# Three gate units inside the last retention chunk, row sums of the down weights on VectorE, and the tail's diagonals earlier

## The reference

```
h = x + W_out( sig(g_A) * Ret(RMSNorm(x)) + sig(g_B) * MLA(RMSNorm(x)) )
h = h + (silu(g) * u) @ w_down,  g, u = split(RMSNorm(h) @ w_gate_up)      # D_FF = 2816
y = RMSNorm(h) * norm_final_w
```

## Time and profile before

| | |
|---|---|
| median of 3 runs | 2051.46 us (2051.01 to 2053.17) |
| the profiled execution | 2048.32 us, its span 2046.5 us |
| TensorE (PE) busy | 1968.6 us, 96% |
| VectorE (DVE) / ScalarE (ACT) / GpSimd (POOL) busy | 1367.6 / 831.7 / 621.8 us |
| mean granted TensorE clock | 0.985 of full |
| chain that ended last | PE 81%, DVE 12%, issue 3%, ACT 2% |
| DMA | 276.29 MB, 135 GB/s mean |

### The profile page before, as it was taken

The page is one execution under the profiler, slowest core; times in us unless marked ns, Lnnn a source line. Parts: engine busy times, 40 slices in busy tenths (PEclk is TensorE's granted clock), DMA queues, the critical chain, the costliest instruction groups (busy, mean ns, idle before and its releaser), DMA issues.

```text
span 2046.5 us, 35899 instructions
## 1 busy us (share of the span) xinstructions
PE 1968.6 (96%) x14476; PEld 1900.1 (93%) x14476; DVE 1367.6 (67%) x2020; ACT 831.7 (41%) x1426; POOL 621.8 (30%) x470
## 2 busy tenths in 40 slices
PE   8999999999999989899999979999999999999997
PEld 8978888889989989899999979999999999999997
DVE  6567776765666556866668896756556565686775
ACT  6334445442222235455554425633333333333342
POOL 0110000001345442225133232144444444370342
PEclk9999999999999989999999989999999999999998
DMA  8301010152354565854755543222323222564322
GB/s 315 113 25 33 25 33 25 32 207 64 122 175 158 170 242 190 297 187 159 243 205 209 182 136 131 78 77 91 107 80 112 91 97 100 198 243 170 109 83 88
DMA packets 112724, 276.29 MB, mean 135 GB/s; under 512 B 13232, under 2 KB 29552, under 8 KB 106032
## 3 DMA queue, kind: packets, MB, share of 16 engines
q1 hardware_dynamic: 112560, 273.99, 38.2%
HBM read 188.79 MB, written 85.16 MB: 134 GB/s over the span
## 4 chain that ended last, share of the span: by engine, by line
PE 81%; DVE 12%; issue 3%; ACT 2%; DMA 1%; POOL 1%; SPq 0%; DVEq 0%; ACTq 0%; POOLq 0%
PE ps L1209 24%; PE ps L1210 24%; PE ps L1211 24%; PE ps L1304 1%; PE ps L1402 1%; DVE tmp L2297 1%; DVE negmax L2519 1%; DVE t_lo L2290 1%; PE ps L1310 1%; PE ps L1518 1%; PE ps L1465 1%; DVE pt_lo L2290 1%; PE ps L1461 1%; PE ps L1462 1%; DVE s_lo L2290 1%
## 5 line engine op out<-in xcount | busy, mean ns | idle before, releaser
L1209 PE MATMUL ps<-s_hi,t_hi 128*128 128x272 f32 x1344 | 393.1, 292 | 20.4 <-DVE s_lo L2290 19.4
L1210 PE MATMUL ps<-s_hi,t_lo 128*128 128x272 f32 x1344 | 391.2, 291 | 0.0
L1211 PE MATMUL ps<-s_lo,t_hi 128*128 128x272 f32 x1344 | 389.9, 290 | 0.0
L1209 PE MATMUL ps<-sx_hi,t_hi 128*128 128x272 f32 x1232 | 357.3, 290 | 3.0 <-ACT p L2106 2.5
L1210 PE MATMUL ps<-sx_hi,t_lo 128*128 128x272 f32 x1232 | 357.2, 290 | 0.0
L1209 PEld LDWEIGHTS ps<-s_hi,t_hi 128*128 128x128 f32 x1344 | 256.9, 191 | 23.0 <-DVE s_lo L2290 13.4
L1210 PEld LDWEIGHTS ps<-s_hi,t_lo 128*128 128x128 f32 x1344 | 256.7, 191 | 0.0
L1211 PEld LDWEIGHTS ps<-s_lo,t_hi 128*128 128x128 f32 x1344 | 256.7, 191 | 0.0
L1211 PE MATMUL ps<-sx_lo,t_hi 128*128 128x272 f32 x880 | 255.5, 290 | 0.0
L1209 PEld LDWEIGHTS ps<-sx_hi,t_hi 128*128 128x128 f32 x1232 | 234.9, 191 | 3.4 <-issue 3.3
L1210 PEld LDWEIGHTS ps<-sx_hi,t_lo 128*128 128x128 f32 x1232 | 234.5, 190 | 0.0
(11 more groups left out here) (281 smaller groups left out, 4883.4 us busy)
## 6 DMA issues: line engine op xcount, KB each, us to landing
t_row<-in_weights SPq DMA_DIRECT2D x48, 512.0 KB, 5.9
s_raw<-s_x SPq DMA_DIRECT2D x21, 1088.0 KB, 5.7
w_stage<-in_weights SPq DMA_DIRECT2D x35, 512.0 KB, 3.9
s_y<-hg SPq DMA_DIRECT2D x44, 272.0 KB, 2.1
d_raw<-s_y SPq DMA_DIRECT2D x7, 1632.0 KB, 8.9
raw<-in_weights SPq DMA_DIRECT2D x22, 512.0 KB, 4.4
hg<-in_weights SPq DMA_DIRECT2D x22, 512.0 KB, 4.6
d_raw<-s_y SPq DMA_DIRECT2D x7, 1360.0 KB, 6.0
```

Source lines behind the costliest of these rows:

```text
L1209: nc.tensor.matmul(out, wh, xh, start=start, stop=False, skip_group_check=onto)
L1210: nc.tensor.matmul(out, wl, xh, start=False, stop=False, skip_group_check=onto)
L1211: return nc.tensor.matmul(out, wh, xl, start=False, stop=stop, skip_group_check=onto)
```

## The change

Four edits in one.

1. `retention_steps` puts three gate units U of octet 0 into the last head: U0 after Z(6), U1 and U2 after Z(7), ahead of Z(8). In the first two octets the units use other bank pairs (`octet_banks`: 3, 0, 2, 1 for p = 0 to 3). The roundings of their weights and operand are spread over chunks 4 to 8 on ScalarE and VectorE, the first operand is loaded one chunk earlier, the weight rows 3 and 1 are loaded half by half, and the last state is stored before the last transposed tile.
2. In the last gate-up pair ScalarE rounds the first down operand after p5's copy instead of before it, and SyncE issues that operand's load before the pair's stores and the residual's load after the second operand's.
3. The down weights' sums T3, T2, T4, T1 go from GpSimd to VectorE, inside its loop; the operand of step 1 is split before the loop.
4. In the tail VectorE makes the diagonals before accumulations that stood ahead of them, and the scalings are spread between the accumulations.

```diff
@@ retention_steps
         if c:
             steps.append(("Z", c - 1))
+        if head + 1 == RH and c == 7:
+            steps.append(("U", 0))
     steps += [("F", *unit) for unit in fill]
+    if head + 1 == RH:
+        steps += [("U", 1), ("U", 2)]
     return steps + [("Z", 8)]
...
+        def octet_banks(o, p):
+            b = 2 * ((3, 0, 2, 1)[p] if o in (GATE_RET, GATE_A) else p)
+            return ps[:, b:b + 2, 0:QUARTER]
@@ first_loads, SyncE
-                elif c == 6:
+                elif c == 5:
...
-                    for r in (3, 1):
-                        for half in range(2):
+                    for half in range(2):
+                        for r in (3, 1):
                             row_load(0, r, half)
@@ SyncE, last head
+                        if s[1] == 8:
+                            sp.wait_ge(state_f, 9 * h + 9)
+                            sp.dma_start(o["state_s"][:, h, :], s_sample[h % 2][:, :]).then_inc(state_out[h % 2], 16)
                         sp.wait_ge(zt_copy, n + 1)
...
@@ SyncE, after the pairs
+                    sp.wait_ge(q_done, last + 1)
+                    down_operand_load(0)
                 gated_store(pair)
...
             down_operand_load(1)
+            for p in range(4):
+                sp.wait_ge(h_out[p], H_OUT + 64)
+            residual_load(C11)
@@ octet_unit, TensorE: banks of units 0 to 3 of octet 0 are free when
                 elif s == 0:
                     if p == 0:
+                        pe.wait_ge(p_free, own[-1])
+                    elif p == 1:
                         pe.wait_ge(sc_mid, 9 * RH)
                         pe.wait_ge(z_copy, 9 * RH)
-                    elif p == 1:
-                        pe.wait_ge(zt_copy, 9 * RH)
-                        pe.wait_ge(kd_copy, 9 * RH)
                     elif p == 2:
                         pe.wait_ge(state_f, 9 * RH)
                     else:
-                        pe.wait_ge(p_free, own[-1])
+                        pe.wait_ge(zt_copy, 9 * RH)
+                        pe.wait_ge(kd_copy, 9 * RH)
@@ ScalarE: weights of units 0, 1 after B(4), B(5), of 2, 3 after B(8); operand parts after A(7) and Z(5)
+                if n >= 9 * RH - 5 and n != 9 * RH - 3 and n != 9 * RH - 2:
+                    weights_octet({9 * RH - 5: 0, 9 * RH - 4: 1, 9 * RH - 1: 2}[n])
                 if n == 9 * RH - 1:
+                    weights_octet(3)
@@ VectorE: low halves after B(5), B(6), B(8), N(8); the operand's after N(6)
+                        if n in (9 * RH - 4, 9 * RH - 3, 9 * RH - 1):
+                            weights_octet_low({9 * RH - 4: 0, 9 * RH - 3: 1, 9 * RH - 1: 2}[n])
@@ ScalarE, last pair
                 part(p5, pair, "Z")
...
+                elif not more:
+                    for part_of in range(2):
+                        down_operand_high(0, part_of)
@@ VectorE, down
+            for part_of in range(3):
+                down_operand_low(1, part_of)
             for u in range(LAST_STEP):
+                g, n = divmod(u, UNITS)
+                if n < 4:
+                    down_sums(g, "T3", n)
+                    down_sums(g, "T2", n)
+                if 8 <= n < 12:
+                    down_sums(g, "T4", n - 8)
+                if 13 <= n < 17:
+                    down_sums(g, "T1", n - 13)
@@ VectorE, tail (the new order)
+            accumulate_part(0, 1)
             final_diagonal(0)
+            accumulate_part(0, 2)
+            final_scale(0, 0)
             accumulate_part(0, 3)
...
+            accumulate_part(1, 1)
+            final_scale(0, 5)
+            final_diagonal(1)
+            final_scale(0, 6)
+            accumulate_part(1, 2)
...
+            accumulate_part(1, 3)
+            for t in range(2, 5):
                 final_scale(1, t)
+            final_diagonal(2)
```

More of the change, by code:

```diff
@@ L1146, in gated_store @@
                         operand_store(6, e, y_s4)
+            last = 7 * (UP_PAIRS - 1)
             for pair in range(UP_PAIRS - 1):
@@ L1424, in _, with octet_unit @@
                         last.then_inc(p_done, 1)
+            def octet_unit(o, s, p):
+                n, j = UNITS * o + 4 * s + p, STEPS * o + s
+                opens = s in OPENING_STEPS
+                pe.wait_ge(ot_low, n + 1)
+                if s == 0 and o:
+                    pe.wait_ge(o_read, reads_until(o - 1, 4 * C12 + ((1, 3, 2, 0)[p] if o == GATE_B else p)))
+                elif s == 0:
+                    if p == 0:
+                        pe.wait_ge(p_free, own[-1])
+                    elif p == 1:
+                        pe.wait_ge(sc_mid, 9 * RH)
+                        pe.wait_ge(z_copy, 9 * RH)
+                    elif p == 2:
+                        pe.wait_ge(state_f, 9 * RH)
+                    else:
+                        pe.wait_ge(zt_copy, 9 * RH)
+                        pe.wait_ge(kd_copy, 9 * RH)
+                elif s < 4:
+                    pe.wait_ge(o_copy, 12 * o + 4 * (s - 1) + p + 1)
+                elif s == 4 and o in GATES:
+                    pe.wait_ge(c_act, 16 * o + p + 1)
+                else:
+                    pe.wait_ge(o_read, reads_until(o, 4 * (s - 4) + p))
+                th, tl = t_hi[n % 4], t_lo[n % 4]
+                for half in range(2):
+                    cols = slice(QUARTER * half, QUARTER * (half + 1))
+                    for k in range(4):
+                        if p == 0 and half == 0 and k % 2 == 0:
+                            pe.wait_ge(so_low, 2 * j + k // 2 + 1)
+                        last = product(octet_banks(o, p)[:, half, :], th[:, k, :], tl[:, k, :],
+                                       s_hi[j % 3][:, k, cols], s_lo[j % 3][:, k, cols], k == 0 and opens, k == 3, not opens)
+                last.then_inc(oct_done, 1)
             for h in range(RH):
@@ L1474, in _ @@
                         last.then_inc(zt_done, 1)
[L1478 to L1488, removed]
-                    elif p == 1:
-                        pe.wait_ge(zt_copy, 9 * RH)
-                        pe.wait_ge(kd_copy, 9 * RH)
-                    elif p == 2:
-                        pe.wait_ge(state_f, 9 * RH)
-                    else:
-                        pe.wait_ge(p_free, own[-1])
[L1496 to L1507, removed]
-                        last = product(ps[:, 2 * p + half, 0:QUARTER], th[:, k, :], tl[:, k, :],
-                                       s_hi[j % 3][:, k, cols], s_lo[j % 3][:, k, cols], k == 0 and opens, k == 3, not opens)
-                last.then_inc(oct_done, 1)
             def square_sums(i):
@@ L2195, in _ @@
                     weights_high(n, "B")
-                else:
-                    for part_of in range(2):
-                        down_operand_high(0, part_of)
                 act.wait_ge(q_done, 7 * pair + 4)
@@ L2605, in _ @@
                                                 rstd[0:L, n % 2, :], ALU.subtract, ALU.mult).then_inc(z_norm, 1)
-            for part_of in range(2):
-                operand_octet_low(0, part_of)
+                        if n == 9 * RH - 1:
+                            weights_octet_low(3)
+                        if n == 9 * RH - 3:
+                            for part_of in range(2):
+                                operand_octet_low(0, part_of)
             def weights_low(pair, step):
@@ L2831, in down_weights_low, with down_sums @@
                     d_weights(dw_hi, u).rearrange("p k c -> p (k c)")).then_inc(dw_low, 1)
+            def down_sums(g, name, p):
+                b11, b12, b21, b22 = [d_rows[r][p // 2][:, p % 2, 0:DOWN_GROUPS[g] * P] for r in range(4)]
+                if name == "T3":
+                    for r in (1, 3):
+                        dve.wait_ge(row_in[r][p // 2], 16 * (OCTETS + g + 1))
+                    nc.vector.tensor_tensor(b12, b22, b12, ALU.subtract).then_inc(dw_sum, 1)
+                elif name == "T2":
+                    dve.wait_ge(dw_low, UNITS * g + p + 1)
+                    dve.wait_ge(dw_sum, dw_sum_at(g, "T3", p))
+                    nc.vector.tensor_tensor(b11, b12, b11, ALU.add).then_inc(dw_sum, 1)
+                elif name == "T4":
+                    dve.wait_ge(row_in[2][p // 2], 16 * (OCTETS + g + 1))
+                    dve.wait_ge(dw_low, UNITS * g + 8 + p + 1)
+                    dve.wait_ge(dw_sum, dw_sum_at(g, "T2", p))
+                    nc.vector.tensor_tensor(b12, b21, b11, ALU.subtract).then_inc(dw_sum, 1)
+                else:
+                    dve.wait_ge(dw_low, UNITS * g + 4 + p + 1)
+                    dve.wait_ge(dw_sum, dw_sum_at(g, "T4", p))
+                    nc.vector.tensor_tensor(b11, b22, b11, ALU.subtract).then_inc(dw_sum, 1)
             def down_operand_low(j, part_of):
@@ L2968, in final_scale @@
                                                    ps[:, 2 + 2 * i, 0:QUARTER], ALU.mult, ALU.mult).then_inc(scaled, 1)
+            for part_of in range(3):
+                down_operand_low(1, part_of)
```

(4 more changed lines are left out.)

96 lines of the change are left out of this document (32 added, 64 removed).

## The result

The changed kernel takes **2035.82 us** (median of 4 runs, 2034.43 to 2037.54), the kernel before, beside it on the same chip, 2052.32 us (4 runs, 2051.01 to 2054.84). The profiled executions stand closer: 2037.54 us (span 2035.7, clock 0.986) against 2048.32 (2046.5, 0.985), 10.8 us.

The account below looks back on a forecast made before the run. TensorE was taken to bound the kernel, leaving only its holes and half clock to win. Gains of 1.0 + 2.5 + 4.4 + 4.3 = 12.2 us from 2051.46 gave 2039.3 us, range 2034.5 to 2045.

Parts of the forecast that it names:

- signs of being wrong: Copy starting after 764, sums above 1.5 us, new TensorE wait at down units 3 to 6, over one new half-clock stretch.
- Part 1: Retention into first octet: unit 4 ends 2.1 us sooner, minus 1.1 us half clock; 1.0 us gained (1.5 lost to 4).
- What bounds, and the price of half clock: Whole kernel: TensorE busy 1968.6 of 2046.5 us; only holes and half clock winnable; 3.41 us busy half clock costs 1.55.
- rival A: Retention: its hole comes back whole before unit 4 with more half clock, worth -1.5 us, total 2041.8; chance 0.14.
- Part 2: Last gate-up pair: p5 copied once its bank is full, operand load issued earlier; 2.5 us gained (2.0 to 2.6).
- Part 3: Down stage: row sums on VectorE remove a 2.9 us wait and 1.5 us of clock; 4.4 us gained (1 to 4.5).
- B: Down stage: VectorE's sums are hindered by late rows, gain shrinks to 0 or 1 us, total 2043.3; chance 0.10.
- D: Down stage: VectorE becomes the bound; sums of 2.5 us eat all 12.2 us, at 2.9 total 2057; chance 0.03.
- Part 4: Tail: earlier diagonals save 2.25, 1.28 and 0.3 us of waits, plus 0.5 us of clock; 4.3 us gained (3 to 5).
- the base: Whole kernel before the change: median 2051.46 us, from which the forecast gain was subtracted.

Follow-up runs that it names:

- two experiments: Changed kernel with the whole retention edit taken back: 2034.74 us, ratio 0.991; kernel before with the retention edit alone: 2053.94 us, ratio 1.0004.
- the two experiments on it: Changed kernel with operand and weights rounded ahead of the quadrant copy: 2037.03 us; the same with the last store between units 1 and 2: 2034.75 us.

## Why the prediction was nearly right

The time lies in the range, but two of the prediction's own signs of being wrong came: the copy began after 764 (764.69), and there is more than one new half-clock stretch (767.43, 1276.01, 1293.08). Part 1 and the two stretches gave less than forecast and parts 2 to 4 more, and that these nearly cancel in the profiles (10.8 us against 12.2) is luck.

**What bounds, and the price of half clock.** Right. Each hole that came back in the down stage brought a stretch of 3.41 us of half clock, and cost its own length plus some 1.5 us there: 2.73 + 1.55 and 2.62 + 1.55 (positions differ by 4.4 us in both). In their profiles both cost 1.6 us more in the tail, which no term of the sum has: what is undone in one stage can move the half clock of a later one.

**Part 1, +1.0 forecast, -0.6 by the profile, nothing by two experiments.** The mechanism was right step by step. Unit 0 was forecast at 746.7 and started at 748.02, of which 1.1 us is from before the edit. From there unit 0 took 3.2 us rather than 3.0 and chunk 8 with the transposes behind it 2.1 rather than 1.5, so the last transposed block was stored at 760.27, 0.8 us late. ScalarE's rows:

```profile
759.73 0.52 ACT L1972 ACTIVATE zt<-ps,gains 128x64 f32<-128x64 f32 x2 [5.26 <-PE ps L1521]
764.69 0.62 ACT L2032 ACTIVATE hg<-ps 128x544 f32<-128x544 f32 x1 [4.44 <-DMA yr_spill<-zt]
```

The store took 3.9 us, near my 3.6. The copy was forecast at 762.0 and came at 764.69, past the bound of 764, of which again 1.1 is older. The term that was mis-sized is the clock's, "I charge 1.1 us for it (0 to 3)": it was 5.71 x 0.454 = 2.6 us. A stop that I expected at the operand's second half didn't come (0.18 us), which hid most of the late copy. That the hole has the forecast 4.8 us is luck: the copy is late, but so is unit 3, and the first low half takes 1.28 us instead of the 2.28 of before, since GpSimd's sums are over by 766.5. This is rival A in kind. I named the queue behind the copy but had its price wrong: by the two experiments on it, the store is only one of two covers, the other being VectorE's halves beside GpSimd at 2.4 us.

**Part 2, +2.5 forecast.** The wait for `p` is gone. The step's reasoning gave the gain to "p5 copied as soon as its bank is full". The runs give it to the load: with the load early the order on ScalarE is worth nothing, and without it the new order loses 3.6 us in the profile. ScalarE's last pair, the answer to the earlier trace rows:

```profile
1779.83 0.63 ACT L2124 ACTIVATE p<-ps 128x544 f32<-128x544 f32 x1 [2.37 <-PE ps L1223]
1780.35 2.10 ACT L2148 ACTIVATE d_hi<-d_raw 128x1088 fp32r<-128x1088 f32 x2
```

**Part 3, +4.4 forecast, 7.4 together with part 2 against 6.9.** Right. VectorE's rows in the down stage, where the earlier trace rows stood, and the tile of the rows:

```profile
1802.67 0.95 DVE L2861 TENSOR_TENSOR d_row<-d_row,d_row 128x768 f32<-128x768 f32 x1
1803.72 0.96 DVE L2865 TENSOR_TENSOR d_row<-d_row,d_row 128x768 f32<-128x768 f32 x1
1804.60 0.95 DVE L2310 TENSOR_TENSOR dw_lo<-d_row,dw_hi 128x768 fp32r<-128x768 f32 x1
1805.47 0.71 DVE L2973 TENSOR_TENSOR hg<-hg,ps 128x544 f32<-128x544 f32 x1
```

```profile
L2310 DVE TENSOR_TENSOR dw_lo<-d_row,dw_hi x56: 816/884/2111, 1786.3 to 2006.3; 128x768 fp32r<-128x768 f32 x28, 128x640 fp32r<-128x640 f32 x28
...
L2861 DVE TENSOR_TENSOR d_row<-d_row,d_row x8: 815/884/951, 1799.2 to 1928.3; 128x768 f32<-128x768 f32 x4, 128x640 f32<-128x640 f32 x4
```

A sum costs 0.95 us of 0.96 forecast, a unit 3.43 of 3.6. Rivals B and D needed 2.5 us or a late row; neither came. The experiment with the operand in the loop shows that the step named as an aside, the split before the loop, is needed as much as the move of the sums.

**Part 4, +4.3 forecast, 6.8 by position, 5.5 by the experiment.** The waits went as forecast, with a little more at the third diagonal:

```profile
2028.59 0.72 PE L1649 MATMUL ps<-fin_diag,ones 128*128 128x272 f32 x2 [1.23 <-DVE fin_diag L2992]
```

2.25 + 1.28 + (1.92 - 1.23) = 4.2 us against my 2.25 + 1.28 + 0.3. The clock was mis-sized: I let the drop of 2016.88 stay and gave it back 0.5 us; there was none before 2030.36, worth 4.57 x 0.454 = 2.1. In before it began ahead of the hole, which is why I kept it. That part 4 alone took it away isn't shown: with the new tail it came back in the two runs that undid half of part 3.

**The base and the sum.** From profile to profile the gain is 10.8 us, 1.4 less than forecast; from median to median it is 16.5, 4.3 more, of which 0.9 is the base (2051.46 was shown, 2052.32 measured beside the result; later comparisons gave 2052.3 to 2053.2). Undone one at a time, the parts cost 0 or less (part 1), 3.8 (part 2's load), 4.8 to 6.4 (part 3) and 5.5 us (part 4), medians against the 2036.26 of the changed kernel, each good to 1 or 2 us: 14 to 16 of some 16.5. The surplus over the forecast thus lies in parts 2 to 4, mostly, it seems, in the half clock that goes with their holes. Open: why the changed kernel has the half clock at 1276 and 1293.

## What to carry to other kernels

A hole before a unit has as many causes as there are queues that end near it: before an edit is priced, write down when each of them would be ready with the first removed. Here 2.2 us off the store bought 1.5 us at most, inside the spread, and with the operand's place in three queues it bought 5 us. Price a hole with the clock behind it, and test an edit of two halves by undoing each: in the last pair one half was idle, in the down stage neither worked alone.

## What the runs showed of the hardware

A half clock can follow work in which the profile shows TensorE never idle (its busy time is modelled). In both kernels this burst of passes of one column stands ahead of 1276; TensorE's timeline after, then the window around it:

```profile
1272.38 2.23 PE L1533 MATMUL ps<-ones,sq 128*128 128x1 f32 x20
```

```profile
1268.00:1280.00 12.00, 12.00 (x89) 11.94 (x87) 6.02 (x9) 6.92 (x11) 0.00 (x0) 0.86 0.12 46
```

and the same window of the kernel before, whose burst starts 0.06 us later:

```profile
1268.00:1280.00 12.00, 12.00 (x100) 11.91 (x99) 7.31 (x11) 8.21 (x12) 0.00 (x0) 1.00 0.16 63
```

Busy is 12.00 of 12.00 in both, the clock 0.86 and 1.00. All eleven profiles that have the retention edit and the whole burst show a half-clock stretch that starts between 1268.9 and 1277.1, and seven of them the second, near 1293; the kernel before with the retention edit alone has both (1275.44, 1292.50). Neither of the two without that edit shows one there (before has none, retention undone has one at 1219.29 instead), nor the one with the burst thinned. So the 3.0 us may belong to part 1, by way of where the burst falls; the two experiments on part 1, which find it worth nothing, include them. Executions of the changed kernel differ by 3 us, with a clock between 0.986 and 0.989. The Trainium skill ("TensorE: Matmul & The Clock Gate", Part 1) says that the number of slow products at a kernel's start varies from run to run of one kernel; the two profiles of the changed kernel differ in that manner at 129.13 and 139.38, where one has half clock and the other none, but a stretch that comes back in eleven profiles isn't chance alone. What sets it stays open.
